# Chunked RWKV-7 scan: side work of a pass in twelve pieces, one beside each slot of the inverse

## What is computed

```python
def _wkv7_step(S, inp):
    r_t, w_t, k_t, v_t, aa_t, bb_t = inp
    sa = jnp.einsum('zbhij,zbhj->zbhi', S, aa_t)
    S = S * w_t[..., None, :] + sa[..., :, None] * bb_t[..., None, :] + v_t[..., :, None] * k_t[..., None, :]
    y = jnp.einsum('zbhij,zbhj->zbhi', S, r_t)
    return S, y
```

## Time and profile before

| | |
|---|---|
| median of 3 runs | 4833.85 us (4824.33, 4833.85, 4844.38) |
| profiled execution, its own time | 4831.92 us |
| its span, first to last instruction | 4829.9 us |
| mean granted TensorE clock | 0.948 of full speed |
| the scan within it | from about 2470 to 3572 us |
| busy, share of the span | TensorE 88%, weight loads 74%, VectorE 41%, ScalarE 28%, GpSimd 27% |

### The profile page before, as it was taken

How to read it: one execution, slowest core, us unless ns; L and a number is a source line. 1 busy time by engine, 2 the same in 40 slices (tenths; PEclk the granted TensorE clock), 3 DMA queues, 4 the chain that set the end, 5 groups by cost and what they waited for, 6 DMA issues and landing times. The chain is left out here.

```text
span 4829.9 us, 110845 instructions
## 1 busy us (share of the span) xinstructions
PE 4273.5 (88%) x49032; PEld 3580.1 (74%) x49032; DVE 1956.5 (41%) x3539; ACT 1368.6 (28%) x2860; POOL 1280.9 (27%) x794
## 2 busy tenths in 40 slices
PE   3899888999999997997957888888778999999997
PEld 2688856888888886775747777777755888888885
DVE  3011054244243442217137676776733254152441
ACT  2111065211111112236215555555532211011110
POOL 2111032311111114210125555555512311111110
PEclk6899999999999998998979999999989999999998
DMA  4211243311313213221232222222232311313214
GB/s 131 64 53 62 69 129 75 126 36 51 111 40 95 67 48 95 69 76 40 88 91 67 65 75 71 65 75 59 61 113 80 122 40 52 110 39 102 61 50 162
DMA packets 402634, 372.29 MB, mean 77 GB/s; under 512 B 63056, under 2 KB 370512, under 8 KB 399984
## 3 DMA queue, kind: packets, MB, share of 16 engines
q1 hardware_dynamic: 390320, 354.75, 23.8%
q10 hardware_dynamic: 11840, 10.49, 0.6%
HBM read 257.68 MB, written 107.48 MB: 76 GB/s over the span
## 5 line engine op out<-in xcount | busy, mean ns | idle before, releaser
L422 POOL TENSOR_TENSOR f_wlow<-f_raw,f_whigh 128x1024 fp32r<-128x1024 f32 (+1 forms) x152 | 360.1, 2369 | 1670.5 <-ACT f_whigh L493 1670.5
L478 PE MATMUL f_ps<-fx_hh,f_whigh 128*128 128x512 f32 (+1 forms) x2112 | 529.1, 359 | 0.0
L478 PE MATMUL f_ps<-fx_hl,f_whigh 128*128 128x512 f32 (+1 forms) x2112 | 528.2, 358 | 0.0
L478 PE MATMUL f_ps<-fx_hh,f_wlow 128*128 128x512 f32 (+1 forms) x2112 | 527.6, 358 | 0.0
L493 ACT ACTIVATE f_whigh<-f_raw 128x1024 fp32r<-128x1024 f32 (+1 forms) x152 | 156.5, 1029 | 923.4 <-PE f_ps L478 894.9
L478 PEld LDWEIGHTS f_ps<-fx_hl,f_whigh 128*128 128x128 f32 x2112 | 348.2, 188 | 66.3
L478 PEld LDWEIGHTS f_ps<-fx_hh,f_wlow 128*128 128x128 f32 x2112 | 347.9, 188 | 66.2
L478 PEld LDWEIGHTS f_ps<-fx_hh,f_whigh 128*128 128x128 f32 x2112 | 348.4, 188 | 65.5
L478 PE MATMUL f_ps<-mo_oh,f_whigh 128*128 128x512 f32 (+1 forms) x1440 | 360.8, 359 | 26.0 <-POOL f_wlow L422 26.0
L1606 PE MATMUL sc_inv_ps<-sc_tf,sc_bl 64*64 64x64 f32 x6400 | 282.8, 223 | 107.8 <-DVE sc_tf L1966 60.1
L478 PE MATMUL f_ps<-mo_ol,f_whigh 128*128 128x512 f32 (+1 forms) x1440 | 360.0, 358 | 0.0
(11 more groups left out here) (267 smaller groups left out, 8381.3 us busy)
## 6 DMA issues: line engine op xcount, KB each, us to landing
f_xo<-xres SPq DMA_DIRECT2D x64, 640.0 KB
xres<-f_xo SPq DMA_DIRECT2D x56, 640.0 KB, 2.9
f_raw<-in_ffn_w_gate SPq DMA_DIRECT2D x44, 512.0 KB
f_raw<-in_ffn_w_up SPq DMA_DIRECT2D x44, 512.0 KB
sc_rk<-rkvl SPq DMA_DIRECT2D x80, 256.0 KB
rkvl<-ri_ot SPq DMA_DIRECT2D x28, 640.0 KB, 2.9
f_raw<-in_ffn_w_down SPq DMA_DIRECT2D x32, 448.0 KB
qkv_raw<-in_na_w_qkv SPq DMA_DIRECT2D x24, 512.0 KB, 5.5
```

The costliest lines, as they stand in the source:

```text
L422: nc.gpsimd.tensor_tensor(wlow[:, m % 2, 0:kt], raw[:, 0:kt], whigh[:, m % 2, 0:kt].bitcast(F32), ALU.subtract).then_inc(cut_lo, 1)
L478: last = nc.tensor.matmul(ps[:, m % 2, n, 0:count], w[:, m % 2, k], x[:, k, t0:t0 + count], start=(k == 0 and w is whigh and x is xh), sto ...
```

## The change

The loop over s becomes a loop over the twelve slots n = 3s + part on every engine, with at most one or two pieces of side work beside each. Gram, turn and y are cut into halves of two chunks; `gram_out` is cut into bm and ga and, one slot later, nr (`inclusive_out`); the tanhs, the gates and the sums are cut in two (`decay_tanh`, `rate_tanh`, `decay_gate`, `rate_gates`, `sums`, `sums_back`). A half posts its flag only with the second half and waits only ahead of the first. On GpSimd `directions` and `receptance` move between the two directions' levels, and the wait for `d_cum` moves from `levels` to `directions`. What is computed, and the buffers, stay as they were.

```diff
-                def gram(G, z):
+                def gram(G, z, half):
                     r = G % 4
-                    if z == 0:
+                    if half == 0 and z == 0:
                         pe.wait_ge(d_rec, G + 1)
                         pe.wait_ge(g_r, G + 1)
                         if G >= 2:
                             pe.wait_ge(a_turn[1], G - 1)
-                    else:
+                    elif half == 0:
                         pe.wait_ge(d_gram[0], G + 1)
-                    for s in range(U):
+                    for s in (2 * half, 2 * half + 1):
...
-                    last.then_inc(pe_gram[z], 1)
+                    if half:
+                        last.then_inc(pe_gram[z], 1)
...
                 for I in range(-3, NG):
-                    for s in range(U):
+                    for n in range(3 * U):
+                        s, part = divmod(n, 3)
                         if group(I):
-                            x_product(I, s)
-                        inverse(I + 1, 3 * s)
-                        if group(I):
-                            u_product(I, s)
-                        if s == 0 and group(I + 3):
+                            if part == 0:
+                                x_product(I, s)
+                            elif part == 1:
+                                u_product(I, s)
+                            else:
+                                s_product(I, s)
+                        if n in (0, 1) and group(I + 2):
+                            gram(I + 2, 0, n)
+                        if n == 2 and group(I + 3):
                             lora(I + 3)
-                        if s == 2 and group(I + 1):
-                            turn(I + 1, 0)
-                        inverse(I + 1, 3 * s + 1)
-                        if group(I):
-                            s_product(I, s)
-                        if s < 2 and group(I + 2):
-                            gram(I + 2, s)
-                        if s == 1 and group(I - 1):
-                            y_products(I - 1)
-                        if s == 2 and group(I + 1):
-                            turn(I + 1, 1)
-                        if s == 3 and group(I + 3):
+                        if n in (3, 6) and group(I + 2):
+                            gram(I + 2, 1, n // 3 - 1)
+                        if n in (4, 5) and group(I - 1):
+                            y_products(I - 1, n - 4)
+                        if n in (7, 8) and group(I + 1):
+                            turn(I + 1, 0, n - 7)
+                        if n in (9, 10) and group(I + 1):
+                            turn(I + 1, 1, n - 9)
+                        if n == 11 and group(I + 3):
                             bonus(I + 3)
-                        inverse(I + 1, 3 * s + 2)
+                        inverse(I + 1, n)
...
                 for I in range(-3, NG):
-                    for s in range(U):
-                        if group(I):
+                    for n in range(3 * U):
+                        s, part = divmod(n, 3)
+                        if group(I) and part == 0:
                             x_copy(4 * I + s)
-                        p_copy(I + 1, 3 * s)
-                        if group(I):
+                        if group(I) and part == 1:
                             u_copy(4 * I + s)
+                        p_copy(I + 1, n)
+                        if group(I) and part == 1:
                             fade_state(4 * I + s)
-                        if s == 3 and group(I + 1):
+                        if n == 2 and group(I + 3):
+                            decay_tanh(I + 3)
+                        if n == 3 and group(I + 3):
+                            rate_tanh(I + 3)
+                            decay_gate(I + 3)
+                        if n == 4 and group(I + 3):
+                            rate_gates(I + 3)
+                        if n == 5 and group(I - 1):
+                            y_copy(I - 1)
+                        if n == 6 and group(I + 3):
+                            exps(I + 3)
+                        if n == 8 and group(I + 1):
+                            turn_copy(I + 1, 0)
+                        if n == 10 and group(I + 1):
                             turn_copy(I + 1, 1)
-                        p_copy(I + 1, 3 * s + 1)
-                        if group(I + 3):
-                            if s == 0:
-                                tanhs(I + 3)
-                            if s == 1:
-                                gates(I + 3)
-                            if s == 2:
-                                exps(I + 3)
-                        if s == 1 and group(I - 1):
-                            y_copy(I - 1)
-                        if s == 2 and group(I + 1):
-                            turn_copy(I + 1, 0)
-                        p_copy(I + 1, 3 * s + 2)
...
                 for I in range(-3, NG):
-                    for s in range(U):
-                        g = 4 * I + s
-                        level_out(I + 1, 3 * s)
-                        level_out(I + 1, 3 * s + 1)
-                        if group(I):
-                            state_out(g)
-                        if s < 2 and group(I + 2):
-                            gram_out(I + 2, s)
-                        level_out(I + 1, 3 * s + 2)
-                        if s == 1 and group(I + 3):
+                    for n in range(3 * U):
+                        s, part = divmod(n, 3)
+                        if group(I) and part == 2:
+                            state_out(4 * I + s)
+                        level_out(I + 1, n)
+                        if n == 0 and group(I + 2):
+                            bonus_out(I + 2)
+                        if n == 1 and group(I + 2):
+                            gram_out(I + 2, 0)
+                        if n == 2 and group(I + 2):
+                            inclusive_out(I + 2, 0)
+                        if n == 4 and group(I + 3):
                             sums(I + 3)
-                        if s == 2 and group(I + 3):
+                        if n == 5:
+                            if group(I + 3):
+                                sums_back(I + 3)
+                            if group(I + 2):
+                                inverse_init(I + 2, 0)
+                        if n == 6 and group(I + 2):
+                            gram_out(I + 2, 1)
+                        if n == 7 and group(I + 2):
+                            inclusive_out(I + 2, 1)
+                        if n == 9 and group(I + 2):
+                            inverse_init(I + 2, 1)
+                        if n == 10 and group(I + 3):
                             bonus_rows(I + 3)
+                        if n == 11 and group(I + 3):
                             keys(I + 3)
-                        if s == 3 and group(I + 3):
                             queries(I + 3)
-                            bonus_out(I + 3)
-                        if s >= 2 and group(I + 2):
-                            inverse_init(I + 2, s - 2)
...
                 for I in range(-3, NG):
-                    for s in range(U):
-                        if s == 1 and group(I + 2):
-                            first_level(I + 2, 0)
-                            levels(I + 2, 0)
-                        if s == 2 and group(I + 2):
-                            first_level(I + 2, 1)
-                            levels(I + 2, 1)
-                        if s == 1 and group(I + 3):
-                            directions(I + 3)
-                        if s == 3 and group(I + 3):
-                            receptance(I + 3)
-                        if s == 0 and group(I + 2):
-                            bonus_add(I + 2)
+                    if group(I + 2):
+                        bonus_add(I + 2)
+                        first_level(I + 2, 0)
+                        levels(I + 2, 0)
+                    if group(I + 3):
+                        directions(I + 3)
+                        receptance(I + 3)
+                    if group(I + 2):
+                        first_level(I + 2, 1)
+                        levels(I + 2, 1)
```

More of the change, by code:

```diff
@@ L1569, in gram, with turn @@
                                                         rec[rows, r, z, u, 2:4].rearrange("p a n -> p (a n)"), start=True, stop=True)
-                    last.then_inc(pe_gram[z], 1)
-                def turn(G, z):
+                    if half:
+                        last.then_inc(pe_gram[z], 1)
+                def turn(G, z, half):
                     r = G % 4
-                    if z == 0:
+                    if half == 0 and z == 0:
                         pe.wait_ge(v_in[r], 32 * (G // 4 + 1))
@@ L1579, in turn @@
                             pe.wait_ge(a_y, G - 1)
-                    elif group(G + 1):
+                    elif half == 0 and group(G + 1):
                         pe.wait_ge(d_gram[1], G + 2)
-                    elif G:
```

(32 more changed lines are left out.)

7 lines of the change are left out of this document (4 added, 3 removed).

## The result

The changed kernel takes 4931.8 us in the median against 4831.9 for the kernel before on the same chip: ratio 1.0205, 95% interval 1.0181 to 1.0229, 100 us slower. The profiled execution has a span of 4930.8 us.

The account below looks back on a forecast made before the run. TensorE's work, 17.9 of a 25.7 us pass, plus waits and "issue" set the pass. Work and new waits 25.6 plus 2.2 of "issue" give 27.8, +2.1 a pass, +78 us over some 37 passes: 4912, range 4790 to 4980.

Parts of the forecast that it names:

- The old waits: TensorE's waits in slots 1, 3, 4, 6, 9 and 10 go, a gain of 4 us a pass, counted in full.
- issue: TensorE stalls with no cause shown by the profile, 3.7 us a pass before; 2.2 taken to stay.
- Slot 3 (nr): First half of Gram of direction 1 waits for nr, now posted behind slot 2's sum and transposes: 2.0 us.
- Slot 4 (tanh): First half of y waits for the second tanh, now posted after slot 3's copy of P: 1.4 us.
- Slot 6 (state): x(2) waits for the state, which VectorE now writes behind the two scans: 1.65 us.
- Slot 8 (u_copy): TensorE waits for u_copy(2), which now stands behind the exponentials: 0.8 us.
- Slot 0 (d_rec): First half of Gram of direction 0 waits for d_rec, since keys and queries now end the pass: 0.4 us.
- Slot 11 (tb): Bonus waits for tb, which VectorE does after inverse_init(1) and slot 10's sum: about 1.1 us.
- Rival C: GpSimd becomes the bound: kd's lag goes through inverse_init(1) into bonus and x, 0.7 us a pass, 4938; chance 0.11.
- The prediction's upper end: Instruction cache refills go by instruction count alone, so all 3.7 us a pass of TensorE's unexplained stalls stay: 4965.
- Rival A: The gaps close as meant, new waits 1 to 3 us less; decided at slot 3; say 4755, chance 0.18.
- Rival B: It cancels: TensorE's unexplained stalls are swallowed whole by the new waits, 25.6 us a pass against 25.7, 4828; chance 0.13.

Follow-up runs that it names:

- three repairs: The changed kernel with nr back in slot 1, the two scans in slot 3 and both tanhs in slot 2: 4830.1 us, ratio 0.9992.
- tb in slot 8: The changed kernel with nr in slot 1, scans in slot 3, tanhs in slot 2, GpSimd's record products last, and tb in slot 8, not 10: 4806.5 us, ratio 0.9929.
- the filled wait: The changed kernel with four more matmuls on constants ahead of TensorE's wait for tb in slot 11, their result unused: 4900.4 us, ratio 1.0137.

## Why the prediction was right

Forecast 4912, measured 4932, inside the range of 4790 to 4980 and on the forecast's side; +2.1 us a pass was forecast, +2.57 came. The order of the flags was foreseen; that the sum came so near is in part luck, since its terms were off both ways. The old waits that it let go, 4 us, were 2.5 in the view of waits (2.9 less the 0.4 in slot 0, which stayed), and the work of a pass, 17.9, is 19.2 when waits and "issue" are taken off (19.6 after the change). Against that, the new waits came to 7.0 (7.4 less the same 0.4) instead of 7.75, and "issue" fell by 2.4 instead of some 1.6. Step by step:

- **The mechanism was right.** The moved flags are late, each in the place named. The runs that put one back give 68, 34 and 50 us, and all three together the whole loss. The smaller ones (u_copy, d_rec) were not put back and rest on the rows of waits alone.
- **Slot 3 (nr), 2.0 forecast:** 63.8 us in 31.9 passes, 2.0. **Slot 4 (tanh), 1.4:** 1.0 to 1.1. **Slot 6 (state), 1.65:** 1.0. **Slot 9 (state), 0.4:** 0.3. **Slot 8 (u_copy), 0.8:** 0.4. **Slot 0 (d_rec), 0.4:** 0.2. In all of these the walk was right or too long, by 0.65 in slot 6; stalls that TensorE has anyway may fall into the waits, which no run shows.
- **Slot 11 (tb), 1.1 forecast, 1.9 measured:** the mis-sized term. It took tb at 0.75 us from a moment when GpSimd stood idle. Moved to slot 10 it lies beside the level blocks. The text had checked GpSimd's chain for being late and called its cost nothing. For the scans it did note that a GpSimd instruction beside them lengthens them; it did not ask the same of tb. Rival C had the right engine and the wrong mechanism: VectorE's wait for it was 5.9 us in the whole stretch.
- **"Issue", 2.2 us of the old 3.7 taken to stay, 1.3 measured.** More was swallowed than taken. The prediction's upper end, refills by instruction count alone, would have left all of it; in the changed kernel most of it is gone, and the repaired kernels, whose waits are short, show it again at 3.3 (three repairs) and 3.6 (tb in slot 8). That the long waits cover it is read from this, and that these stalls are refills no row shows. The Trainium skill (Advanced Engine Details and Errata, section ISA Cache), which the prediction named there, gives TensorE 128 KB and only the other engines the 32 KB of two such lines, and says nothing of how often refills come; it gives no ground for the upper end on TensorE.
- **The clock had no term.** It stayed at 0.99 in the rows, and the forecast kept it there; the fall to 0.94 costs about the 33 us that the filled wait gives back. Less "issue" and shorter waits on the one side, more of tb and of the clock and a smaller gain from the old waits on the other, partly cancel.
- **Rival A** decided at slot 3, as the text said: Gram starts 2 us behind x. As a statement about the order it was half right: with its flags in time, and tb and GpSimd's records moved as well, the finer order is 0.7% faster than the kernel before. There TensorE still stands 3.6 us a pass on "issue" and 2.7 on other engines.
- **Rival B** said that "issue" would be swallowed whole and the two cancel: two thirds were swallowed.

## What to carry to other kernels

When work is spread evenly over an engine's gaps, look up for each piece which flag it waits for and where in its own engine's order that flag is now posted: a half put one slot behind its producer waits longer than the gap it fills. Before an instruction is moved, look at what the other engine runs at its new place as well as at its length in the old one. And don't add up the gains of single repairs: here 152 us were worth 103 together, since each repair uncovered stalls, and each raised the same clock.

## What the runs showed of the hardware

- VectorE's instructions with two inputs in SBUF (tb, keys) that start beside a long tensor operation of GpSimd stand until it is through, and end 0.55 us after it: keys 3.27 us instead of 0.68 beside the 2.89 us of blocks. Scans are lengthened too (0.90 instead of 0.69 in the median with tb in slot 8), and in four passes of the kernel before so was a copy with one input in SBUF (L1869, up to 1.05 instead of 0.17). Transposes (one input, 0.44 each) and sums and masks that read PSUM (0.29, 0.68) kept their lengths.
- The other way round, a GpSimd instruction that starts while VectorE is at such a one is lengthened: the record product behind tb took 1.72 us instead of 1.28, and in the four passes of the run with blocks held back until tb in which keys started 0.11 to 0.16 us ahead of them, keys kept its 0.68 and the blocks took 3.26 to 3.31 us instead of 2.89. The Trainium skill (SBUF — State Buffer, section SBUF: two separate sides) says that VectorE and GpSimd have a pair of SBUF ports in common, that a VectorE instruction with two SBUF inputs and a GpSimd instruction that reads SBUF exclude each other there, and that the one that starts first keeps the pair to its end; the trace agrees in both directions.
- The granted clock fell to its lower level after TensorE had stood some 1.3 to 2.3 us before bonus (15 times) and 1.9 us before Gram of direction 1 (10 times), not in every pass; four idle-filling matmuls a pass raised the mean from 0.94 to 0.99, and the kernel was 33 us faster.
